# GpSimd issues the transfers of each expert's second matrix, SyncE keeps the first

## What is computed

```
logits = (hf @ router_w + router_b)
top_val, top_idx = lax.top_k(logits, TOP_K)          # TOP_K = 4 of 32
gate = jax.nn.softmax(top_val, axis=-1)
...
gu = xk @ w1[e] + b1[e]                              # w1[e]: 1024 x 2048, 8 MB
g_lin, u_lin = gu[:, :D_FF], gu[:, D_FF:]
act = (u_lin + 1) * (g_lin * jax.nn.sigmoid(SWIGLU_ALPHA * g_lin))   # both clamped at 7
return act @ w2[e] + b2[e]                           # w2[e]: 1024 x 1024, 4 MB
```

## Time and profile before

| | before |
|---|---|
| median of 3 runs | 1155.3 us (1153.67 to 1158.33) |
| the profiled execution | 1155.17 us, of which its span is 1153.3 us |
| bytes moved | 457.59 MB, mean 397 GB/s |
| PE busy, share of the span | 85% |
| DVE, ACT, POOL busy | 31%, 12%, 1% |
| mean granted TensorE clock | 0.945 |

### The profile page before, as it was taken

One profiled execution on the slowest core, in us unless ns is written; L12 is line 12 of the kernel. 1 busy time (PEld: TensorE's weight loads), 2 busy tenths in 40 slices (PEclk: granted clock), 3 DMA queues, 4 the chain that ended last, 5 costly groups with the idle time before them and its releaser, 6 DMA issues.

```text
span 1153.3 us, 20722 instructions
## 1 busy us (share of the span) xinstructions
PE 981.4 (85%) x7543; PEld 446.5 (39%) x7544; DVE 357.6 (31%) x963; ACT 141.9 (12%) x336; POOL 15.7 (1%) x26
## 2 busy tenths in 40 slices
PE   4999989979899778899887999787989887888755
PEld 2776343334443323443333443323444323232322
DVE  1788884321123222122221222222123322122222
ACT  2234540000100000100000001000010100000002
POOL 1000300000000000000000000000000000000000
PEclk9999989989899998999998999998989998979977
DMA  9994989999999999999999999999999999999994
GB/s 357 248 388 169 385 315 414 419 420 421 413 387 421 423 421 423 422 421 421 422 422 422 422 406 424 422 422 422 422 406 407 422 422 422 422 421 422 422 421 190
DMA packets 82864, 457.59 MB, mean 397 GB/s; under 512 B 9439, under 2 KB 25895, under 8 KB 30062
## 3 DMA queue, kind: packets, MB, share of 16 engines
q1 hardware_dynamic: 81568, 456.44, 97.4%
q10 hardware_dynamic: 1262, 0.69, 0.2%
HBM read 456.05 MB, written 1.05 MB: 396 GB/s over the span
## 4 chain that ended last, share of the span: by engine, by line
PE 57%; DMA 27%; SPq 5%; DVE 5%; issue 5%; ACT 1%; POOL 0%; DVEq 0%; ACTq 0%; POOLq 0%
DMA ring<-in_exp_w 27%; PE bank L1349 24%; PE bank L1372 13%; SPq L326 5%; PE bank L1209 5%; PE bank L1328 3%; PE bank L1239 2%; PE bank L1303 2%; PE bank L1191 1%; PE bank L1359 1%; PE bank L1326 1%; PE bank L1340 1%; DVE scratch L1006 1%; PE bank L1154 1%; PE bank L1161 1%
## 5 line engine op out<-in xcount | busy, mean ns | idle before, releaser
L1349 PE MATMUL bank<-ring,xg 128*32 128x256 f32 (+2 forms) x3200 | 444.7, 484 | 57.9 <-DMA ring<-in_exp_w 57.8
L1349 PEld LDWEIGHTS bank<-ring,xg 128*32 128x32 f32 (+2 forms) x3200 | 167.7, 129 | 320.2 <-issue 172.5
L1372 PE MATMUL bank<-ring,actT 128*32 128x512 f32 (+2 forms) x1056 | 217.8, 616 | 20.4 <-DMA ring<-in_exp_w 12.3
L1372 PEld LDWEIGHTS bank<-ring,actT 128*32 128x32 f32 (+2 forms) x1056 | 76.5, 134 | 139.3 <-issue 110.0
L557 ACT ACTIVATE act<-scratch 128x128 f32<-128x128 f32 (+2 forms) x66 | 25.6, 388 | 829.8 <-DVE scratch L1006 828.3
L1006 DVE TENSOR_SCALAR scratch<-bank 128x128 f32<-128x128 f32 (+2 forms) x66 | 25.3, 383 | 312.8 <-PE bank L1349 312.8
L995 DVE SCALAR_TENSOR_TENSOR acc<-bank,gate,acc 128x512 f32<-128x512 f32 x136 | 93.1, 743 | 55.3 <-PE bank L1328 43.9
L1025 DVE TENSOR_TENSOR ysb<-bank,g2half 128x512 f32<-128x512 f32 x29 | 20.1, 692 | 215.4 <-PE bank L1372 215.4
L1303 PEld LDWEIGHTS bank<-onehot_bf,arena 128*128 128x128 bf16 x1584 | 54.2, 100 | 23.2 <-issue 23.0
L1328 PE MATMUL bank<-ysb,onehotT 64*128 64x512 f32 x232 | 59.1, 629 | 3.3 <-DVE ysb L1025 2.1
L1303 PE MATMUL bank<-onehot_bf,arena 128*128 128x32 bf16 (+2 forms) x1584 | 57.7, 193 | 0.8 <-issue 0.8
(11 more groups left out here) (238 smaller groups left out, 496.3 us busy)
## 6 DMA issues: line engine op xcount, KB each, us to landing
ring<-in_exp_w SPq DMA_DIRECT2D x396, 1024.0 KB, 24.2
ring<-in_ada_w SPq DMA_DIRECT2D x24, 1024.0 KB, 12.5
ring<-in_conf_pw_w SPq DMA_DIRECT2D x12, 1024.0 KB, 10.5
acc<-in_x SPq DMA_DIRECT2D x1, 1024.0 KB, 5.0
out<-acc SPq DMA_DIRECT2D x2, 512.0 KB, 3.1
ysb<-in_ada_b SPq DMA_DIRECT2D x8, 64.0 KB, 2.7
ffn_rows<-in_final_norm_g ACTq DMA_DIRECT2D x1, 512.0 KB, 8.6
b1f<-in_exp_b SPq DMA_DIRECT2D x1, 256.0 KB, 4.0
```

What stands on the lines that cost most here:

```text
L1349: ins = mm(up_to(m, n, r), xg[:, b, k, 0:m], wk[:, at:at + span(m)], start=False, stop=(k == KT - 1))
L1372: ins = mm(dst, actT[:, f % (2 * q), at:at + m], wk[:, f % 2 * D + r * H:f % 2 * D + (r + 1) * H], start=(f < sides), stop=(f >= KT - sides))
```

## The change

The second matrix of each expert but the first is taken from SyncE and issued by GpSimd, on GpSimd's queue, with four semaphores of its own (`landed_w2`). SyncE's `expert` loops over the eight chunks of the first matrix alone. Each issue waits for the same value of `used` as before, the slots and sizes are the same, and TensorE's program differs only in the semaphore that it waits on ahead of a chunk of down. GpSimd loads the expert's number from the same tables as SyncE and has loops of its own.

```diff
+        landed_w2 = [sem(f"landed_w2_{n}") for n in range(NCH - KT)]
...
             def expert(i, e):
-                for q in range(NCH):
+                for q in range(KT):
 
                     sp.wait_ge(used, i * NCH + (CH_EXP + q - RING + 1))
-                    if q < KT:
-                        dst = w_slot(q)
-                        src = w1_rows[bass.ds(e, 1), q, :, :].rearrange("e p n -> (e p) n")
-                    else:
-                        dst = w_slot(q)
-                        src = w2_rows[bass.ds(e, 1), q - KT, :, :].rearrange("e p n -> (e p) n")
-                    sp.dma_start(dst, src).then_inc(landed[q], 16)
+                    sp.dma_start(w_slot(q), w1_rows[bass.ds(e, 1), q, :, :].rearrange("e p n -> (e p) n")
+                                 ).then_inc(landed[q], 16)
 
             expert(0, 0)
+            for q in range(KT, NCH):
+                sp.wait_ge(used, CH_EXP + q - RING + 1)
+                sp.dma_start(w_slot(q), w2_rows[0, q - KT, :, :]).then_inc(landed[q], 16)
...
+            def expert(i, e):
+                for q in range(KT, NCH):
+
+                    pool.wait_ge(used, i * NCH + (CH_EXP + q - RING + 1))
+                    pool.dma_start(w_slot(q), w2_rows[bass.ds(e, 1), q - KT, :, :].rearrange("e p n -> (e p) n")
+                                   ).then_inc(landed_w2[q - KT], 16)
+
+            pool.wait_ge(s_next, 1)
+            e1 = pool.value_load(second_e[0:1, 0:1], min_val=0, max_val=E - 1)
+            expert(1, e1)
+            pool.wait_ge(s_seq, 4)
+            with pool.Fori(2, E) as i:
+                e = pool.value_load(nexte[0:1, bass.ds(i, 1)], min_val=0, max_val=E - 1)
+                expert(i, e)
...
+            def arrived_w2(i, q):
+                pe.wait_ge(landed_w2[q], i * 16)
+                return w_slot(KT + q)
...
-                    wk = arrived(i, KT + f // 2) if f % 2 == 0 else wk
+                    if f % 2 == 0:
+                        wk = arrived(0, KT + f // 2) if first else arrived_w2(i, f // 2)
```

More of the change, by code:

```diff
@@ L269, in up_to @@
             return bank[2 * r + n][:, :] if m == WIDE else bank[n][m * r:m * r + m, 0:span(m)]
+        w1_rows = exp_w1[0].rearrange("e (k p) n -> e k p n", p=P)
+        w2_rows = exp_w2[0].rearrange("e (q p a) n -> e q p (a n)", p=P, a=2)
         @block.sync
@@ L311, in _ @@
                         sp.dma_start(b2f[64 * r:64 * r + E, :], exp_b2[0, :, r * H:(r + 1) * H]).then_inc(s_b2, 16)
-            w1_rows = exp_w1[0].rearrange("e (k p) n -> e k p n", p=P)
-            w2_rows = exp_w2[0].rearrange("e (q p a) n -> e q p (a n)", p=P, a=2)
             def expert(i, e):
-                for q in range(NCH):
+                for q in range(KT):
                     sp.wait_ge(used, i * NCH + (CH_EXP + q - RING + 1))
-                    if q < KT:
-                        dst = w_slot(q)
-                        src = w1_rows[bass.ds(e, 1), q, :, :].rearrange("e p n -> (e p) n")
-                    else:
-                        dst = w_slot(q)
-                        src = w2_rows[bass.ds(e, 1), q - KT, :, :].rearrange("e p n -> (e p) n")
-                    sp.dma_start(dst, src).then_inc(landed[q], 16)
+                    sp.dma_start(w_slot(q), w1_rows[bass.ds(e, 1), q, :, :].rearrange("e p n -> (e p) n")
+                                 ).then_inc(landed[q], 16)
             expert(0, 0)
+            for q in range(KT, NCH):
+                sp.wait_ge(used, CH_EXP + q - RING + 1)
+                sp.dma_start(w_slot(q), w2_rows[0, q - KT, :, :]).then_inc(landed[q], 16)
             sp.wait_ge(s_next, 1)
@@ L391, in _ @@
             spread(g2full[:, :], modrow[1][64:128, :], s_rows2)
+            def expert(i, e):
[10 more added lines that the diff above has]
+                expert(i, e)
+            more = pool.value_load(extras[0:1, 0:1], min_val=0, max_val=EXTRA)
+            with pool.If(more > 0):
+                with pool.Fori(0, more) as i:
+                    e = pool.value_load(eidx[0:1, bass.ds(i, 1)], min_val=0, max_val=E - 1)
+                    expert(i + E, e)
         @block.scalar
@@ L1351, in up, with down @@
                     ins.then_inc(used, 1)
-            def down(i, i2, m):
+            def arrived_w2(i, q):
+                pe.wait_ge(landed_w2[q], i * 16)
+                return w_slot(KT + q)
+            def down(i, i2, m, first=False):
                 q = KT * m // WIDE // 2
@@ L1444, in item_0 @@
                 pe.wait_ge(xg_ready, 2)
-                either(pe, w0, SIZES[0], lambda m: down(0, 0, m))
+                either(pe, w0, SIZES[0], lambda m: down(0, 0, m, True))
                 return after
```

## The result

The changed kernel takes 1189.7 us in the median (1186.1 to 1192.4 over two sets of runs), against 1154.7 us before in the same set. So it is 35.0 us slower in the median. The ratio on record is 1.0281, with a 95% interval of 1.0252 to 1.0310; the two medians divided give 1.0303. The forecast was 1195 us, 40 slower, with a range of 1166 to 1245. One execution of the first set ran at a granted clock of 0.557 and took 1653 us; it is left out here (the median would be 1190.4 with it). The profiled execution is the fastest of its set: 1186.07 us with a span of 1184.4, which is 31.1 over the span of before. The sum is checked against these 31.1.

The account below looks back on a forecast made before the run. It took the transfers, in the order they are needed, to bound this stage. Terms 0 + 34 (four WIDE items) + 6 (end) gave +40 us on the 1155.3 median, so 1195 us, range 1166 to 1245.

Parts of the forecast that it names:

- No gain from the issues, no higher rate: SyncE's four removed issues per item, 0.34 us each, would give nothing; two queues would not make the DMA engines faster.
- The engines share evenly: Two full queues take turns on the DMA engines, so the second matrix gets about half of each engine.
- The shift, 9.9 us or 4.0 chunks: Up's last chunk lands twelfth, not eighth; TensorE falls 9.9 us or 4.0 chunks behind the transfers, free while DMA stays busy.
- The four WIDE items, +34 us: Where TensorE is slower than the transfers, 6 chunks queued, not 10; DMA idles some 9.9 us at each, +34 in all.
- The end, +6 us: At the program's end all of down lies behind up's last chunk: 8 to 10 us after the last landing, not 4.0.
- (a): GpSimd's time for one issue, 0.34 to 1.4 us: taken as 0 cost, with +10 kept for the range's end.
- (b): Bytes of GpSimd's transfers, rows of 8 KB as now: taken as 0 cost; if cut smaller, up to +105 us.
- (c): GpSimd's queue's share of the engines, taken as 50%: at 40% the loss is +28, below one third +70 and more.
- No change: Rival: engines serve by arrival, WIDE items have more reserve, or only issue time moves; 1150 to 1161 us, chance 0.07.
- faster: Rival: a second queue fills the dips behind the WIDE items, at most 5.4 us and 1 at the end; 1149, chance 0.04.
- A costly software path: Rival: the same shift plus longer issue, smaller or slower packets on GpSimd's queue; 1210 to 1300 us, chance 0.28.
- Small share: Rival: engines favour SyncE's queue, so landing order stays near the order of use; 1161 to 1180 us, chance 0.09.

## Why the prediction was right, step by step

*No gain from the issues, no higher rate.* Right. SyncE was 24 us ahead; taking four issues from it gave nothing. Two queues together move 422 GB/s, as one does.

*The engines share evenly.* Right: 54.7% and 46.7%, and chunks 4.97 us apart. The rows that I had read it from the earlier trace rows show 76.4% and 25.3%, over a stretch with one queue alone for part of it; the half was a choice, and it came true. The Trainium skill, page "DMA: Bandwidth & Descriptors", section "Queues, rings and completion order", has the round-robin, and the trace agrees. Its section "Issuing engines are not separate DMA queues" is right in that nothing gets faster, but it doesn't follow that nothing changes: the run is 2.8% slower.

*The shift, 9.9 us or 4.0 chunks.* Right in kind, too large. The step that was off is that the four chunks "are through after 8 chunk times (19.9 us)" and the last chunk of up "then lands as the twelfth, not the eighth". I counted from one moment, but the four slots come free one after another, and their transfers start only then. GpSimd issued them for item 15 from 617.7 to 622.8, and the last one landed 19 us after that, at 641.9, seven after the last chunk of up (634.9). So of the 12.5 us from there to the end of down, part still went to this item: 2, 3, 3 and 4 chunks of the next had landed, 3.0 on average and not 4.0. Item 15 is no exception: in 26 of the 32 items on two queues the last chunk of the second matrix lands behind the last of up, so that up's last chunk is the twelfth in six alone. The sign of being wrong at the root, up complete before the second chunk of down, shows in five of them.

*The four WIDE items, +34 us.* Measured +27.4. My bookkeeping was loose: 52.7 - 42.2 is 10.5 and not 9.9, and for the idle time of before, 5.4 by my own count of the dips and 6.2 measured, I took off 4 x 0.4 and 4 x 1.0. The depth was misread too: when a WIDE item begins, 11 chunks are queued before and 9, 8, 8 and 7 after, where I had 10 and 6. By my depth of 10, but with three chunks landed early and not four, the sum is 4 x (52.7 - 18 x 2.485) = 31.9 us of idle time, less the 6.2 of before, 26 us. That it is these four items and not the two queues as such is shown by the kernels without them: 4.8 us of loss is left.

*The end, +6 us.* Measured +3.7 (3.6 by the idle time of DMA), and at most 4.8 without WIDE items. The wait for the last chunk (1164.69) and the 7.2 us to the end of down are there; the clock was full in this down (3.74 us), where it was 5.41 us before, which the larger of my figures had taken over.

*The sum.* 40 against 31.1 on the profiled execution, which was the fastest of its set, and 35.0 between the medians. The 4 us between these two are open: both executions that were profiled have spans of 1184.4 and 1186.2 us, at clocks of 0.923 and 0.926, and the longer ones, at 0.917, have no trace.

*The costs that no row showed.* (a) An issue takes GpSimd 0.53 us, and nothing waits for it. (b) The packets cost what SyncE's cost: 39.2 against 39.5 us per MB, and one queue of GpSimd's alone ties with the kernel before. (c) The share is even. The values taken were right, and the range was wide on their account. No row of before could tell them, so that all three came out well was in part luck.

*What the profile was to show.* The holes (303 and 302 GB/s where 280 to 300 was said), SyncE's median of 20.2 us to landing, 134 MB on GpSimd's queue, and no wait in down are there. Two were wrong: GpSimd's median to landing is 13.5 us, not 20, since only the last of four chunks waits for three others (9.3, 13.4, 17.2 and 20.9 us in the median for the first to the last, counted from the landings in the trace); and TensorE's waits for up are longer in sum (105.7 against 57.8 us in PE's rows) and singly (3.9 against 1.9), but fewer, 43 and not 67.

*The rivals.* "No change" and "faster" fell with the result. "A costly software path" fell with the kernel that issues all from GpSimd (1.0012) and with ScalarE's hardware queue (1.0345). "Small share" fell with the measured shares.

## What to carry to other kernels

When transfers are the bound, one queue in the order of use is itself a schedule. A second queue doesn't add rate, it shares evenly, and so brings data early that must lie in a buffer while data that is needed comes late. Judge it by how much is queued when the longest stretch of compute begins, not by issue time: here twelve chunks landed too early, over four such stretches, cost 27.4 us, 2.3 each; the end of the program cost another 3.7, and the items between nothing. An engine's total wait for its inputs doesn't rank two kernels; the idle time of the bound does.

## What was not expected of the hardware

GpSimd's queue can carry nearly the whole stream: 403 MB at 422 GB/s, 0.53 us for the issue of 1 MiB, with a time that can't be told from SyncE's (0.9997 to 1.0027). And the share between two queues is even where it can be seen chunk by chunk, 4.97 us a chunk against 2.485 alone; with ScalarE's queue as the second one the page shows the same four holes.
